# A mixture-of-experts layer: each expert's down product moved from two turns behind its gate product to one

## The chip, the cores and the metric

The kernel runs on one core of one Trainium2 chip. The metric is the device time of one execution of the whole layer in microseconds (us), as the median of the runs made. TensorE (PE) does the matrix products, ScalarE (ACT) and VectorE (DVE) work on their operands and results, GpSimd (POOL) issues the gathers and scatters of token rows, and SyncE (SP) issues the loads of weights. The engines run their own queues in order and meet only at semaphores.

## The reference, cut to what matters

One decoder layer on 1024 tokens of width 1024: attention and a short convolution, an output product, then a layer of 32 experts, of which each token uses two. The change touches the experts alone:

```
def expert_block(args):
    xb, e = args
    return (jax.nn.silu(xb @ w_gate[e]) * (xb @ w_up[e])) @ w_down[e]
```

w_gate and w_up are 1024 x 512 for each expert, w_down is 512 x 1024, all in float32. Each row of the result is weighted by the token's weight for that expert and added to the token's output.

## The kernel before, in words

The front of the kernel (attention, convolution, output product, routing) ends about 637 us into the span; `experts` (line 1505) follows, and the change is in it and in `tile_order` (line 66). Each expert takes up to 96 tokens in one block (SLOTS); what goes beyond that has blocks of its own in `spare_blocks` afterwards.

**The weights** come as tiles of 1 MB, 128 partitions x 2048 floats. Tiles 0 to 3 of an expert hold a quarter each of its gate and up weights, tiles 4 and 5 half each of its down weights. `ORDER` lists all 192 tiles, `PLACE` their place in it. Tile number i is loaded by SP into `raw[i % 12]` as soon as tile i - 12 has been used by PE; ACT rounds it to `w_hi[i % 6]` (`split_hi`, L1592), for which tile i - 6 must have been used; DVE writes what the rounding left, `w_lo`, over `raw` (`split_lo`, L1637). PE multiplies high by high, high by low and low by high parts: 12 matmuls of 512 columns for each tile (L1717, L1719, L1721 for gate and up; L1739, L1741, L1743 for down).

**The turns.** All engines run one loop over turns t. In turn t PE does, in this order: gate tile 0 of expert t; the first half of the transposed rows of expert t + 1 (`turn_rows`, L1693, into bank 4); gate tile 1; the transposes of the hidden rows of expert t - 1 (`turn_hid`, L1701, into bank 5); gate tiles 2 and 3; the second half of the rows of expert t + 1; and the two down tiles of expert t - 2. After gate tile 3 and after down tile 5 PE waits for its own last matmul (L1724, L1746) before it tells ACT.

**The hidden rows** of expert e go: gate and up done (`gated`), ACT's silu (L1600), DVE's product with the up half and the weight (`hidden`, L1647), PE's transposes (L1701), ACT's high part (`round_hid`, L1604), DVE's low part (`low_hid`, L1654), and then PE's down product. ACT copies its result out of banks 2 and 3 (`copy_y`, L1610), and POOL adds it to the output in HBM (`scatter`, L1572), one scatter after the other.

**Order in ACT's and DVE's queues.** In each turn the steps are written at places p = 0 to 5, each behind the split of the p-th tile that PE uses in that turn. Before: the rounding of transposed rows at p = 0 and 3, silu and its product at p = 0 and 1, `copy_y` of expert t - 3 at p = 3, `round_hid` and `low_hid` of expert t - 1 at p = 5. The last two turns (t = 32 and 33) hold no gate product, only what is left over.

**Turns with more.** In turns 4, 7 and 10 DVE also makes parts of the table of the spare blocks (behind split p = 2), and in turn 12 PE sums them and waits for DVE to store the result (SPARE_TURN).

Of the kernel before, what the change touches and what calls it, by code (L numbers as in the profile page):

```python
# [46 lines left out]
E = GROUPS * PER_GROUP  # L47
# [18 lines left out]
def tile_order():  # L66

    order = []
    for e in range(E):
        order += [(e, q) for q in range(4)]  # L70
        order += [(e - 2, q) for q in (4, 5)] if e >= 2 else []
    return order + [(e, q) for e in (E - 2, E - 1) for q in (4, 5)]


ORDER = tile_order()
PLACE = {tile: i for i, tile in enumerate(ORDER)}
# [1428 lines left out]
def experts(nc, sem, s):  # L1505
# [18 lines left out]
    y_ready = sem("y_ready")  # L1524
# [4 lines left out]

    def tile_of(t, p):  # L1530

        return PLACE.get((t, p) if p < 4 else (t - 2, p))

    def half(n):

# [14 lines left out]
    with nc.Block() as block:  # L1550
        @block.sync
        def _(sp):
            for i in range(RING, len(ORDER)):
                sp.wait_ge(s.used, i - RING + 1)
                s.load_tile(sp, i)

        @block.gpsimd
        def _(pool):
            last_row = pool.to_reg(T - 1)

            def gather(e):
                pool.wait_ge(rows_turned[1], e - 1)
                pool.indirect_dma_start(  # L1563
                    out=s.rows[e % 2][:].rearrange("p c q -> p (c q)"), out_offset=None, in_=s.xn2_rows,
                    in_offset=bass.IndirectOffsetOnAxis(ap=s.table_i[:, e:e + 1], axis=0),
                    bounds_check=last_row, oob_is_err=False).then_inc(rows_in[e % 2], 16)

            def scatter(e):
                pool.wait_ge(y_ready, e + 1)
                if e >= 1:  # L1570
                    pool.wait_ge(scattered, e * 16)
                pool.indirect_dma_start(  # L1572
                    out=s.out_rows, out_offset=bass.IndirectOffsetOnAxis(ap=s.table_i[:, e:e + 1], axis=0),
                    in_=s.y_sb[e % 2][:], in_offset=None, bounds_check=last_row, oob_is_err=False,
                    compute_op=ALU.add).then_inc(scattered, 16)

            for e in range(E):
                if e + 2 < E:
                    gather(e + 2)
                if e >= 3:  # L1580
                    scatter(e - 3)
            for e in range(E - 3, E):
                scatter(e)
            pool.wait_ge(scattered, E * 16)

        @block.scalar
        def _(act):
            def split_hi(i):
                if i >= HI:
                    act.wait_ge(s.loaded[i % RING], s.landed(i))  # L1590
                    act.wait_ge(s.used, i - HI + 1)
                    act.copy(s.w_hi[i % HI][:], s.raw[i % RING][:]).then_inc(s.hi_ready, 1)  # L1592

            def round_rows(e, n):
                act.wait_ge(rows_turned[n], e + 1)
                act.copy(s.rT_hi[e % 2][:, half(n), :], turned_rows()).then_inc(rT_hi_ready, 1)  # L1596

            def activate(e):
                act.wait_ge(gated, e + 1)
                act.activation(s.silu[:], ps[0:SLOTS, gate_banks(e), :], ACT.Silu).then_inc(silu_ready, 1)  # L1600

            def round_hid(e):
                act.wait_ge(hid_turned, e + 1)
                act.copy(s.hidT_hi[e % 2][:], turned_hid()).then_inc(hT_hi_ready, 1)  # L1604

            def copy_y(e):
                act.wait_ge(down_done, e + 1)
                if e >= 2:
                    act.wait_ge(scattered, (e - 1) * 16)
                act.copy(s.y_sb[e % 2][:].rearrange("p (a n) -> p a n", a=2), ps[0:SLOTS, 2:4, :]).then_inc(y_ready, 1)  # L1610

            round_rows(0, 0)
            round_rows(0, 1)
            for t in range(E + 2):
                for p in range(6):
                    i = tile_of(t, p)
                    if i is not None:
                        split_hi(i)
                    if p == 0 and 1 <= t < E:
                        round_rows(t, 1)  # L1620
                    if p == 0 and 1 <= t <= E:
                        activate(t - 1)
                    if p == 3 and t + 1 < E:
                        round_rows(t + 1, 0)
                    if p == 3 and t >= 3:
                        copy_y(t - 3)
                    if p == 5 and 1 <= t <= E:
                        round_hid(t - 1)
            copy_y(E - 1)

        @block.vector
        def _(dve):
            own = Order(dve, spare_steps)

            def split_lo(i):
                dve.wait_ge(s.hi_ready, i + 1)
                dve.tensor_tensor(s.w_lo[i % RING][:], s.raw[i % RING][:], s.w_hi[i % HI][:].bitcast(F32),  # L1637
                                  ALU.subtract).then_inc(s.lo_ready, 1)

            def low_rows(e, n):  # L1640
                dve.wait_ge(rT_hi_ready, 2 * e + n + 1)
                dve.tensor_tensor(s.rT_lo[e % 2][:, half(n), :], turned_rows(), s.rT_hi[e % 2][:, half(n), :].bitcast(F32),  # L1642
                                  ALU.subtract).then_inc(rT_lo_ready, 1)

            def hidden(e):
                dve.wait_ge(silu_ready, e + 1)
                dve.scalar_tensor_tensor(s.hid[e % 2][:].rearrange("s c p -> s p c"),  # L1647
                                         s.silu[:].rearrange("s (p c) -> s p c", c=FC), s.table_w[:, e:e + 1],
                                         ps[0:SLOTS, gate_banks(e) + 1, :].rearrange("s (p c) -> s p c", c=FC),
                                         ALU.mult, ALU.mult).then_inc(hid_ready, 1)  # L1650

            def low_hid(e):
                dve.wait_ge(hT_hi_ready, e + 1)
                dve.tensor_tensor(s.hidT_lo[e % 2][:], turned_hid(), s.hidT_hi[e % 2][:].bitcast(F32),  # L1654
                                  ALU.subtract).then_inc(hT_lo_ready, 1)

            for t in range(E + 2):
                for p in range(6):
                    i = tile_of(t, p)
                    if i is not None:  # L1660
                        split_lo(i)
                    if t == 0 and p == 1:
                        low_rows(0, 0)
                        low_rows(0, 1)
                    if p == 0 and 1 <= t < E:
                        low_rows(t, 1)
                    if p == 1 and 1 <= t <= E:
                        hidden(t - 1)
                    if p == 3 and t + 1 < E:
                        low_rows(t + 1, 0)  # L1670
                    if p == 5 and 1 <= t <= E:
                        low_hid(t - 1)
                    if p == 2 and t == SPARE_TURN - 8:
                        spare_places(dve, own.then, s, sp_tab)
                    if p == 2 and t == SPARE_TURN - 5:
                        spare_choices(dve, own.then, s, sp_tab)
                    if p == 2 and t == SPARE_TURN - 2:
                        spare_parts(dve, own.then, s, sp_tab)
                        dve.sem_inc(s.table_parts, 1)
                    if p == 2 and t == SPARE_TURN:  # L1680
                        dve.wait_ge(s.table_summed, 2)
                        spare_columns(dve, own.then, s, sp_tab)
                        dve.sem_inc(columns_ready, 1)

        @block.tensor
        def _(pe):
# [69 lines left out]

            turn_rows(0, 0)
            turn_rows(0, 1)
            for t in range(E + 2):
                if t < E:  # L1760
                    gate_up(t, 0)
                if t + 1 < E:
                    turn_rows(t + 1, 0)
                if t < E:
                    gate_up(t, 1)
                if 1 <= t <= E:
                    turn_hid(t - 1)
                if t == SPARE_TURN:
                    pe.wait_ge(y_ready, t - 2)
                    sum_spare()  # L1770
                    pe.wait_ge(columns_ready, 1)
                if t < E:
                    gate_up(t, 2)
                    gate_up(t, 3)
                if t + 1 < E:
                    turn_rows(t + 1, 1)
                if t >= 2:
                    down(t - 2, 4)
                    down(t - 2, 5)

    x = Shared()
    x.scattered = scattered
# [152 lines left out]
```

## Time and profile before

| | |
|---|---|
| median of 3 runs | 1266.44 us (1266.11 to 1274.25) |
| the profiled execution | 1273.75 us, its span 1271.9 us |
| PE busy over the span | 1132.9 us (89%) |
| DVE, ACT, POOL busy | 839.6 us (66%), 652.8 us (51%), 270.4 us (21%) |
| granted TensorE clock, mean | 0.952 |
| weights and rows read from HBM | 240.55 MB |

The profile page gives the busy time of each engine, the span in 40 slices with the granted clock and the DMA share, the chain that ended last, and the costliest groups of instructions. The trace gives single instructions with their start, their duration and, in brackets, how long their engine had been idle and what released it. A row with "x2" or "x3" holds that many instructions back to back, and the duration is of all of them. An instruction's reported duration reaches beyond the start of the next on the same engine, so chains are best counted from start to start.

### The profile page before, as it was taken

The page shows a single profiled execution, that of the slowest core. Times are in us where ns is not written, and L with a number is a line of the kernel's source. Part 1 is how long each engine was busy: PE and PEld are TensorE (multiplying, and loading weights), DVE is VectorE, ACT ScalarE, POOL GpSimd, SP SyncE. Part 2 cuts the span into 40 slices and gives each one's busy share as a digit, 9 for nine tenths or more (in the row PEclk, how much of TensorE's full clock was granted, in tenths as well). Part 3 has the DMA queues.
Part 4 walks back from the last instruction along what each step waited for, and adds up shares of the span by engine and source line. Part 5 has one row for each costly group of instructions (what it writes and reads, how often), then busy time and mean ns, then how long its engine had stood idle before and what let it go on. Part 6 is the DMA issues. An engine that isn't in the chain of part 4 may idle for free. (4 is left out here: it accounts for less than half of the span.)

```text
span 1271.9 us, 15143 instructions
## 1 busy us (share of the span) xinstructions
PE 1132.9 (89%) x5652; PEld 877.5 (69%) x5652; DVE 839.6 (66%) x911; ACT 652.8 (51%) x869; POOL 270.4 (21%) x397
## 2 busy tenths in 40 slices
PE   3789899999999878998389999999999999999983
PEld 3678788888878767886256666666666666666652
DVE  6546546545565445443578989897888888888851
ACT  5334423442343344221337777776676777777641
POOL 2332232323313312000104121111111111111030
PEclk9789899999999988999589999999999999999997
DMA  8002001200020033226769999999999999999931
GB/s 239 2 1 66 18 17 34 67 18 18 19 65 1 1 133 104 109 106 231 277 205 325 353 364 370 368 365 345 365 363 367 367 357 376 368 364 360 368 95 19
DMA packets 88851, 254.07 MB, mean 200 GB/s; under 512 B 13696, under 2 KB 38288, under 8 KB 80592
## 3 DMA queue, kind: packets, MB, share of 16 engines
q1 hardware_dynamic: 81456, 236.23, 50.7%
q0 software_dynamic: 7328, 16.94, 6.0%
q8 instruction: 43, 0.70, 0.2%
q14 instruction: 24, 0.20, 0.0%
HBM read 240.55 MB, written 20.97 MB: 206 GB/s over the span
## 5 line engine op out<-in xcount | busy, mean ns | idle before, releaser
L1637 DVE TENSOR_TENSOR wlo<-raw,whi 128x2048 fp32r<-128x2048 f32 x192 | 433.7, 2285 | 87.0 <-ACT whi L1592 79.1
L1592 ACT CAST whi<-raw 128x2048 fp32r<-128x2048 f32 x186 | 345.7, 1912 | 0.0
L1717 PE MATMUL banks<-whi,rT_hi 128*96 128x512 f32 x512 | 165.7, 405 | 12.2 <-PE banks L1743 8.8
L1719 PE MATMUL banks<-wlo,rT_hi 128*96 128x512 f32 x512 | 160.6, 395 | 0.0
L1721 PE MATMUL banks<-whi,rT_lo 128*96 128x512 f32 x512 | 160.5, 394 | 0.0
L1596 ACT CAST rT_hi<-banks 128x384 fp32r<-128x384 f32 x64 | 30.7, 479 | 180.2 <-PE banks L1693 180.2
L1572 POOL DMA_INDIRECT out<-y_sb,table_i x32 | 54.7, 1709 | 298.3 <-ACT y_sb L1610 298.0
L1717 PEld LDWEIGHTS banks<-whi,rT_hi 128*96 128x96 f32 x512 | 75.9, 163 | 48.3 <-issue 21.6
L1721 PEld LDWEIGHTS banks<-whi,rT_lo 128*96 128x96 f32 x512 | 83.1, 162 | 36.0
L1719 PEld LDWEIGHTS banks<-wlo,rT_hi 128*96 128x96 f32 x512 | 83.0, 162 | 35.8
L1563 POOL DMA_INDIRECT rows<-xn_rows,table_i x30 | 56.8, 1893 | 218.0 <-PE banks L1693 218.0
L920 PE MATMUL banks<-q_hi,xT_hi 128*128 128x384 f32 x256 | 94.7, 370 | 2.3 <-DVE mixT L797 1.3
L1739 PE MATMUL banks<-whi,hidT_hi 128*96 128x512 f32 x256 | 83.8, 409 | 10.3 <-DVE wlo L1637 10.0
L921 PE MATMUL banks<-q_lo,xT_hi 128*128 128x384 f32 x256 | 90.9, 355 | 0.0
L922 PE MATMUL banks<-q_hi,xT_lo 128*128 128x384 f32 x256 | 90.7, 354 | 0.0
L937 PE MATMUL banks<-xT_hi,c_hi 128*128 128x512 f32 x192 | 76.7, 400 | 6.7 <-issue 5.4
L1743 PE MATMUL banks<-whi,hidT_lo 128*96 128x512 f32 x256 | 81.6, 400 | 0.0
L1741 PE MATMUL banks<-wlo,hidT_hi 128*96 128x512 f32 x256 | 81.6, 400 | 0.0
L939 PE MATMUL banks<-xT_hi,c_lo 128*128 128x512 f32 x192 | 74.9, 390 | 0.0
L938 PE MATMUL banks<-xT_lo,c_hi 128*128 128x512 f32 x192 | 74.8, 390 | 0.0
L610 ACT ACTIVATE qk_sq<-banks 128x256 f32<-128x256 f32 x32 | 12.3, 384 | 120.0 <-PE banks L922 120.0
L729 DVE TENSOR_REDUCE qk_ss<-qk_sq 128x4 f32<-128x256 f32 x32 | 13.5, 421 | 78.3 <-ACT qk_sq L610 78.3
(243 smaller groups left out, 2016.2 us busy)
## 6 DMA issues: line engine op xcount, KB each, us to landing
raw<-in_w_gate SPq DMA_DIRECT2D x128, 512.0 KB, 6.5
raw<-in_w_up SPq DMA_DIRECT2D x128, 512.0 KB, 11.7
raw<-in_w_down SPq DMA_DIRECT2D x64, 1024.0 KB, 11.5
q_raw<-in_w_in SPq DMA_DIRECT2D x12, 512.0 KB, 6.0
c_raw<-in_w_in SPq DMA_DIRECT2D x12, 512.0 KB, 3.8
x_all<-in_x SPq DMA_DIRECT2D x8, 512.0 KB, 7.4
wo_raw<-in_w_out SPq DMA_DIRECT2D x2, 2048.0 KB, 11.5
x_again<-in_x SPq DMA_DIRECT2D x8, 512.0 KB, 4.1
```

Of the source, the lines that this page charges most:

```text
L920: pe.matmul(o, s.xT_hi[:, c, cols], s.q_hi[:, c, :], start=(c == 0), stop=False)
L921: pe.matmul(o, s.xT_hi[:, c, cols], s.q_lo[:, c, :], start=False, stop=False)
L922: ins = pe.matmul(o, s.xT_lo[:, c, cols], s.q_hi[:, c, :], start=False, stop=(c == KC - 1))
L937: pe.matmul(ps[:, 6, :], w_hi[:, c, :], s.xT_hi[:, c, cols], start=(c == 0), stop=False)
L1592: act.copy(s.w_hi[i % HI][:], s.raw[i % RING][:]).then_inc(s.hi_ready, 1)
L1637: dve.tensor_tensor(s.w_lo[i % RING][:], s.raw[i % RING][:], s.w_hi[i % HI][:].bitcast(F32), ALU.subtract).then_inc(s.lo_ready, 1)
L1717: pe.matmul(ps[0:SLOTS, bank + g, :], s.rT_hi[e % 2][:, c, :], hi[:, g, c2, :], start=(c == 0), stop=False)
L1719: pe.matmul(ps[0:SLOTS, bank + g, :], s.rT_hi[e % 2][:, c, :], lo[:, g, c2, :], start=False, stop=False)
L1721: ins = pe.matmul(ps[0:SLOTS, bank + g, :], s.rT_lo[e % 2][:, c, :], hi[:, g, c2, :], start=False, stop=(c == KC - 1))
L1739: pe.matmul(ps[0:SLOTS, 2 + n, :], s.hidT_hi[e % 2][:, c, :], hi[:, c2, n * 512:(n + 1) * 512], start=(c == 0), stop=False)
L1741: pe.matmul(ps[0:SLOTS, 2 + n, :], s.hidT_hi[e % 2][:, c, :], lo[:, c2, n * 512:(n + 1) * 512], start=False, stop=False)
L1743: ins = pe.matmul(ps[0:SLOTS, 2 + n, :], s.hidT_lo[e % 2][:, c, :], hi[:, c2, n * 512:(n + 1) * 512], start=False, stop=(c == FC - 1))
```

## The change

The down product of expert e now runs in turn e + 1, not e + 2. The order of the weight tiles moves with it, and so do the steps on ACT, DVE and POOL: `copy_y` takes expert t - 2 at p = 2, `round_hid` and `low_hid` stand at p = 3, behind the rounding of the rows, and POOL scatters expert e - 2. The loops have one turn fewer. No instruction, load or wait is added or removed; the same ones stand in another order.

```
-        order += [(e - 2, q) for q in (4, 5)] if e >= 2 else []
-    return order + [(e, q) for e in (E - 2, E - 1) for q in (4, 5)]
+        order += [(e - 1, q) for q in (4, 5)] if e >= 1 else []
+    return order + [(E - 1, q) for q in (4, 5)]
...
-        return PLACE.get((t, p) if p < 4 else (t - 2, p))
+        return PLACE.get((t, p) if p < 4 else (t - 1, p))
...
-                if e >= 3:
-                    scatter(e - 3)
-            for e in range(E - 3, E):
+                if e >= 2:
+                    scatter(e - 2)
+            for e in range(E - 2, E):
                 scatter(e)
...
-                    if p == 3 and t >= 3:
-                        copy_y(t - 3)
-                    if p == 5 and 1 <= t <= E:
+                    if p == 2 and t >= 2:
+                        copy_y(t - 2)
+                    if p == 3 and 1 <= t <= E:
                         round_hid(t - 1)
...
-                    if p == 5 and 1 <= t <= E:
+                    if p == 3 and 1 <= t <= E:
                         low_hid(t - 1)
...
-                    pe.wait_ge(y_ready, t - 2)
+                    pe.wait_ge(y_ready, t - 1)
...
-                if t >= 2:
-                    down(t - 2, 4)
-                    down(t - 2, 5)
+                if t >= 1:
+                    down(t - 1, 4)
+                    down(t - 1, 5)
```

All loops over `range(E + 2)` become `range(E + 1)`.

**ACT's queue in a steady turn.** Before, from the rounding of the second half of the rows (first row below) to that of the next turn (last row):

```order
L1596 CAST rT_hi_174<-banks 128x384
L1600 ACTIVATE silu<-banks 96x512
L1592 CAST whi_169<-raw_151 128x2048
L1592 CAST whi_170<-raw_152 128x2048
L1592 CAST whi_171<-raw_153 128x2048
L1596 CAST rT_hi_175<-banks 128x384
L1610 COPY y_sb_186<-banks 96x1024
L1592 CAST whi_166<-raw_142 128x2048
L1592 CAST whi_167<-raw_143 128x2048
L1604 CAST hidT_hi_181<-banks 128x384
L1592 CAST whi_168<-raw_144 128x2048
L1596 CAST rT_hi_175<-banks 128x384
```

Now, the same stretch:

```order
L1596 CAST rT_hi_174<-banks 128x384
L1600 ACTIVATE silu<-banks 96x512
L1592 CAST whi_171<-raw_153 128x2048
L1592 CAST whi_166<-raw_142 128x2048
L1610 COPY y_sb_185<-banks 96x1024
L1592 CAST whi_167<-raw_143 128x2048
L1596 CAST rT_hi_175<-banks 128x384
L1604 CAST hidT_hi_181<-banks 128x384
L1592 CAST whi_168<-raw_144 128x2048
L1592 CAST whi_169<-raw_145 128x2048
L1592 CAST whi_170<-raw_146 128x2048
L1596 CAST rT_hi_175<-banks 128x384
```

Gate tiles 1 and 2 stand before the copy of y and gate tile 3 behind it; the hidden rows are rounded before the two down tiles, which had stood in front of them.

**DVE's queue in a steady turn.** Before, from the low part of the rows' first half to the product of the next turn (raw_142 and raw_143 hold the down tiles here, the next two hold gate tiles 0 and 1):

```order
L1642 TENSOR_TENSOR rT_lo_177<-banks,rT_hi_175 128x384
L1637 TENSOR_TENSOR wlo_154<-raw_142,whi_166 128x2048
L1637 TENSOR_TENSOR wlo_155<-raw_143,whi_167 128x2048
L1654 TENSOR_TENSOR hidT_lo_183<-banks,hidT_hi_181 128x384
L1637 TENSOR_TENSOR wlo_156<-raw_144,whi_168 128x2048
L1642 TENSOR_TENSOR rT_lo_177<-banks,rT_hi_175 128x384
L1637 TENSOR_TENSOR wlo_157<-raw_145,whi_169 128x2048
L1647 SCALAR_TENSOR_TENSOR hid_178<-silu,table_w,banks 96x128x4
```

Now, from gate tile 3 (raw_143) to the product of the next turn; the down tiles are in raw_144 and raw_145:

```order
L1637 TENSOR_TENSOR wlo_155<-raw_143,whi_167 128x2048
L1642 TENSOR_TENSOR rT_lo_177<-banks,rT_hi_175 128x384
L1654 TENSOR_TENSOR hidT_lo_183<-banks,hidT_hi_181 128x384
L1637 TENSOR_TENSOR wlo_156<-raw_144,whi_168 128x2048
L1637 TENSOR_TENSOR wlo_157<-raw_145,whi_169 128x2048
L1637 TENSOR_TENSOR wlo_158<-raw_146,whi_170 128x2048
L1642 TENSOR_TENSOR rT_lo_177<-banks,rT_hi_175 128x384
L1637 TENSOR_TENSOR wlo_159<-raw_147,whi_171 128x2048
L1647 SCALAR_TENSOR_TENSOR hid_178<-silu,table_w,banks 96x128x4
```

The low part of the hidden rows (L1654) came behind the down tiles' splits and now comes in front of them.

**ACT's queue at the end.** Before, from the silu of the last expert:

```order
L1600 ACTIVATE silu<-banks 96x512
L1610 COPY y_sb_186<-banks 96x1024
L1592 CAST whi_168<-raw_150 128x2048
L1592 CAST whi_169<-raw_151 128x2048
L1604 CAST hidT_hi_181<-banks 128x384
L1610 COPY y_sb_185<-banks 96x1024
L1592 CAST whi_170<-raw_152 128x2048
L1592 CAST whi_171<-raw_153 128x2048
L1610 COPY y_sb_186<-banks 96x1024
```

Now:

```order
L1592 CAST whi_168<-raw_150 128x2048
L1592 CAST whi_169<-raw_151 128x2048
L1600 ACTIVATE silu<-banks 96x512
L1610 COPY y_sb_185<-banks 96x1024
L1604 CAST hidT_hi_181<-banks 128x384
L1592 CAST whi_170<-raw_152 128x2048
L1592 CAST whi_171<-raw_153 128x2048
L1610 COPY y_sb_186<-banks 96x1024
```

The down tiles of expert 30 (whi_168, whi_169) stood behind a copy of y and now stand ahead of the last silu; those of expert 31 stand behind a copy of y in both.

## Rows read from the trace of the kernel before

**Rows 1.** Page: the span, and each engine's busy time, share, instructions.
```profile
span 1271.9 us, 15143 instructions
PE 1132.9 (89%) x5652; PEld 877.5 (69%) x5652; DVE 839.6 (66%) x911; ACT 652.8 (51%) x869; POOL 270.4 (21%) x397
```

**Rows 2.** Stretch: us; busy PE, PEld, DVE, ACT, POOL (count); clock, DMA share, GB/s.
```profile
700.00:1212.00 512.00, 498.58 (x2342) 343.52 (x2341) 443.49 (x302) 372.95 (x304) 82.53 (x53) 1.00 1.01 364
```

**Rows 3.** Timeline, PE, one steady turn (t = 5): start, us, what, [idle before].
```profile
728.34 0.67 PE L1717 MATMUL banks<-whi,rT_hi 128*96 128x512 f32 x2 [0.30 <-PE banks L1743]
...
734.26 0.49 PE L1701 MATMUL banks<-ident,hid 96*128 96x96 f32 x4
...
740.75 0.68 PE L1739 MATMUL banks<-whi,hidT_hi 128*96 128x512 f32 x2
...
746.82 0.67 PE L1717 MATMUL banks<-whi,rT_hi 128*96 128x512 f32 x2 [0.30 <-PE banks L1743]
```

**Rows 4.** Timeline, ACT, the same turn.
```profile
723.39 5.52 ACT L1592 CAST whi<-raw 128x2048 fp32r<-128x2048 f32 x3
731.69 0.48 ACT L1596 CAST rT_hi<-banks 128x384 fp32r<-128x384 f32 x1 [2.78 <-PE banks L1693]
732.06 1.01 ACT L1610 COPY y_sb<-banks 96x1024 f32<-96x1024 f32 x1
732.97 3.72 ACT L1592 CAST whi<-raw 128x2048 fp32r<-128x2048 f32 x2
...
741.00 0.48 ACT L1596 CAST rT_hi<-banks 128x384 fp32r<-128x384 f32 x1 [2.14 <-PE banks L1693]
```

**Rows 5.** Timeline, DVE, the same turn.
```profile
728.33 1.15 DVE L1647 SCALAR_TENSOR_TENSOR hid<-silu,table_w,banks 96x512 f32<-96x512 f32 x1
729.32 4.47 DVE L1637 TENSOR_TENSOR wlo<-raw,whi 128x2048 fp32r<-128x2048 f32 x2
733.72 0.54 DVE L1642 TENSOR_TENSOR rT_lo<-banks,rT_hi 128x384 fp32r<-128x384 f32 x1
...
739.33 0.55 DVE L1654 TENSOR_TENSOR hidT_lo<-banks,hidT_hi 128x384 fp32r<-128x384 f32 x1
```

**Rows 6.** DMA issues, 700 to 1200 us: count, KB each, median us to landing.
```profile
raw<-in_w_up SPq DMA_DIRECT2D x106, 512.0 KB, 12.5
```

**Rows 7.** Timeline, DVE, turn 7: first table step, and the split behind the last.
```profile
767.65 0.69 DVE L1471 TENSOR_TENSOR which<-own_e,iota_e 128x512 f32<-128x512 f32 x1
...
771.59 2.29 DVE L1637 TENSOR_TENSOR wlo<-raw,whi 128x2048 fp32r<-128x2048 f32 x1
```

**Rows 8.** Timeline, PE, starts of turn 2, of its gate tile 1, and of turn 3.
```profile
670.41 0.68 PE L1717 MATMUL banks<-whi,rT_hi 128*96 128x512 f32 x2
...
675.80 0.70 PE L1717 MATMUL banks<-whi,rT_hi 128*96 128x512 f32 x2 [2.07 <-DVE wlo L1637]
...
691.38 0.67 PE L1717 MATMUL banks<-whi,rT_hi 128*96 128x512 f32 x2 [0.30 <-DVE wlo L1637]
```

**Rows 9.** Timeline, DVE, turns 1 and 2, where it waits.
```profile
667.10 2.28 DVE L1637 TENSOR_TENSOR wlo<-raw,whi 128x2048 fp32r<-128x2048 f32 x1
671.17 0.56 DVE L1642 TENSOR_TENSOR rT_lo<-banks,rT_hi 128x384 fp32r<-128x384 f32 x1 [1.79 <-ACT rT_hi L1596]
```

**Rows 10.** Timeline, all engines, from the end of turn 31 on.
```profile
1229.92 0.62 PE L1743 MATMUL banks<-whi,hidT_lo 128*96 128x512 f32 x2
...
1231.58 3.70 ACT L1592 CAST whi<-raw 128x2048 fp32r<-128x2048 f32 x2
...
1233.51 4.49 DVE L1637 TENSOR_TENSOR wlo<-raw,whi 128x2048 fp32r<-128x2048 f32 x2 [7.13 <-ACT whi L1592]
...
1235.94 1.14 PE L1739 MATMUL banks<-whi,hidT_hi 128*96 128x512 f32 x2 [4.58 <-DVE wlo L1637]
...
1249.74 1.14 PE L1739 MATMUL banks<-whi,hidT_hi 128*96 128x512 f32 x2 [5.41 <-DVE wlo L1637]
...
1257.48 0.63 PE L1743 MATMUL banks<-whi,hidT_lo 128*96 128x512 f32 x2
```

More of the change, by code:

```diff
@@ L1613, in _ @@
             round_rows(0, 1)
-            for t in range(E + 2):
+            for t in range(E + 1):
                 for p in range(6):
@@ L1655, in low_hid @@
                                   ALU.subtract).then_inc(hT_lo_ready, 1)
-            for t in range(E + 2):
+            for t in range(E + 1):
                 for p in range(6):
@@ L1758, in _ @@
             turn_rows(0, 1)
-            for t in range(E + 2):
+            for t in range(E + 1):
                 if t < E:
```

## The prediction

> **What bounds the kernel now.** The page comes first: PE is busy for 89% of the span, DVE for 66%, ACT for 51% [rows 1]. The change lies in the expert turns, so the next view is the busy time of that stretch: from 700 to 1212 us PE is busy for 498.58 of 512 us at a granted clock of 1.00, the 2.4 GHz level, while DVE has 443.49 and ACT 372.95 us [rows 2]. The DMA share is 1.01 there, so a second resource could be the bound; it has to be excluded, which I do below.
>
> Then the timeline of one steady turn. It begins on PE at 728.34 and the next at 746.82, 18.48 us later. Nothing in it waits for another engine; the 0.30 us ahead of each is PE's wait for its own last matmul [rows 3]. Counting from the turn's start, PE turns the hidden rows at 5.92, starts gate tile 2 at about 6.20 and the first down tile at 12.41. The down block holds PE for 18.48 - 12.41 = 6.07 us. Since each gate tile takes a good 2.8 us, gate tile 3 starts at about 9.02. ACT and DVE work ahead of PE: ACT idles 2.78 and 2.14 us in the turn, both times until PE has transposed rows, and never for a landing [rows 4].
>
> So a steady turn is bound by PE's own work, which the change leaves as it is. PE is idle for reasons that the change can touch in two places only: the start (turn 2) and the end (turns 32 and 33).
>
> **The end, before.** The last down matmuls of turn 31 end at 1229.92 + 0.62 = 1230.54. Only then does ACT copy y, and behind that copy stands the high part of the next down tile, from 1231.58; DVE's low part starts at 1233.51 and PE at 1235.94: a gap of 5.40 us. The same is repeated behind expert 30's product, with a gap of 5.41 us; the last product then starts at 1249.74 and ends at 1257.48 + 0.63 = 1258.11, after 8.37 us [rows 10]. Both products begin slow: the first pair of matmuls takes 1.14 us, where pairs at full clock take 0.62. At full clock the block takes 6.07 - 0.30 = 5.77 us [rows 3].
>
> **The end, after.** Expert 30's product runs in turn 31 right behind gate tile 3, its tiles split long before. That makes turn 31 end where turn 31 of before ended, plus one down block: 1230.54 + 6.07 = 1236.61. Then one gap is left. Its chain: ACT's copy of y, released 0.13 us after the last matmul, takes 0.91 us start to start (732.06 to 732.97 [rows 4]); that puts the cast of before at 1.04, as 1231.58 - 1230.54 shows. Now `round_hid` stands between them. It needs PE's transposes, which PE starts 0.30 us after the end and finishes by about 0.8, so ACT doesn't wait; it adds 0.37 us, start to start, of its 0.48. The cast starts at 1.41, and from cast to PE are 4.36 us (1231.58 to 1235.94), so PE starts 5.77 after the end: 1242.38. The product starts slow again, since its gap is as long as the two of before; I take the 8.37 us. End at 1250.75, against 1258.11: **7.36 us less**. What follows (the last copy and scatter) stays.
>
> **The start.** Turn 2 goes from 670.41 to 691.38, 20.97 us, where a steady turn with the same work (it has the down block of expert 0) takes 18.48. The excess, **2.49 us**, is mostly one stall of 2.07 us ahead of gate tile 1 [rows 8]. DVE made gate tile 0's low part at 667.10, then idled 1.79 us until ACT had the next rows at 671.17 [rows 9]; neither had anything to split in that time, as turn 1 has no down tiles. Now it has them. DVE makes them from 667.10 and about 669.3, and gate tile 0 of turn 2 from 671.5. PE runs the down block of expert 0 from 670.41 to 676.48 and needs gate tile 1 at 679.57. DVE has it at about 671.5 + 2.20 + 0.55 + 2.43 = 676.7 (a split 2.20 start to start, rows' low part 0.55, start of a split to its user 2.43). The stall goes; nothing takes its place.
>
> **The price in a steady turn.** Before, `round_hid` and `low_hid` had a whole turn until their down product. Now the chain is: transposes at 5.92, ACT released about 0.53 later at 6.45, the hidden rows' high part 0.37, the down tile's cast and low part 4.36 as at the end, so the tile is ready at 11.18. PE wants it at 12.41. **The margin is 1.23 us**; past it, each of 31 turns pays.
> The rest of the queues, from the same rows. ACT: casts of gate tiles 1 and 2 from -4.95 (723.39) to -1.3; the copy of y then waits until -0.18, when the down block before is done; gate tile 3 from 0.73 to 2.65; the rows at 3.35 as before; `round_hid` at 6.45; three casts from 6.82, 1.84 apart, the last ended at 12.4; the rows of the next turn at 12.66 as before (741.00) [rows 4]. That is 0.3 us spare, and what lies behind it has several. DVE: low part of hidden rows at 6.96, down tiles at 8.75 and 10.95, gate tile 0 at 13.15, rows at 15.35, gate tile 1 at 15.9, product at 18.1 (0.99 to the next [rows 5]), gate tile 2 at 0.6 of the next turn, gate tile 3 at 2.8, ready at 5.2 and wanted at 9.02. DVE still idles some 2.5 us a turn, in front of the hidden rows and of the down tile. I charge a steady turn **0**.
> Turns 4, 7 and 10 put table steps behind gate tile 2, 771.59 - 767.65 = 3.94 us in turn 7, the longest [rows 7]. Gate tile 3 then starts at 6.75 on DVE and is ready at 9.18 for 9.02: 0.16 us, once; the other two are 0.2 us shorter. Then rows and hidden rows (1.1) and the down tile ready at 12.5 for 12.41, another 0.1. I charge **0.2** in all; the bound from the other side is 0.5 for each. Turn 12 stops PE for the table's sum in both kernels; behind it DVE has gate tile 3, rows, hidden rows and a down tile, 2.20 + 0.55 + 0.55 + 2.43 = 5.7 us, and PE needs the last after 12.41 - 6.20 = 6.2. Nothing.
> SP's loads and POOL's scatters: a tile's buffer comes free at the same place as before, twelve tiles ahead, some 37 us. Loads land 12.5 us after issue [rows 6]; ACT now reads the down tile 5.6 us before PE, so some 28 us after its load's issue. The scatter leaves about 3 us earlier in its turn, behind the same gather. Nothing.
>
> **The sum.** 7.36 + 2.49 - 0.2 = 9.65 us. The profiled execution had a span of 1271.9 and a time of 1273.75, 7.3 above the median of 1266.44; the turns are the same work in each, so I take the difference from either: span 1262.2, median **1256.8 us** (0.76% less).
>
> **Bounds.** The last product's speed isn't known: at full clock throughout it takes 5.77, which gives 2.6 less (1254.2); at half throughout 11.5, which gives 3.2 more (1260.0). The Trainium skill, "TensorE: Matmul & The Clock Gate" (section on what's actually happening), says that the same kernel may show 6, 11 or 14 slow matmuls from run to run; these rows don't show such a spread.
>
> **Rivals.**
> *The loads are the bound, and the start's gain is given back* (1259.3). The DMA share of 1.01 speaks for it, ACT's never waiting for a landing against. PE would catch up with the loads and lose the 2.49 us again. The Trainium skill, "DMA: Bandwidth & Descriptors" (where 436 GB/s comes from), puts HBM's limit for a core near 358 GB/s. The trace has 364 over the stretch [rows 2], so it disagrees in size, and by that rule no margin would be left and this rival would be the forecast.
> *The end doesn't shorten* (1264.2): the chain behind expert 31's transposes is longer than read, or expert 30's product stalls in turn 31 for the same 7 us. Against it: its splits stand ahead of the silu in ACT's queue.
> *Slower: the down product waits in each turn.* Place: L1739 of each turn for the low part, L1637. It decides from 1.23 us of lateness; the gains are gone at 1.23 + 9.65 / 31 = 1.54. If the chain were 2.0 us longer, 31 x 0.77 = 24 us, less 9.65: 1281. For it: ACT and DVE are now tied to the transposes only two PE tiles ahead. Against: durations vary by hundredths in these rows, and ACT idles before the transposes come.
> *More than 1% faster* (under 1253.8): the slow start of the last product vanishes and the end has something more.
>
> **How the numbers follow.** Forecast 0.62; start given back 0.14; end not shortened 0.07; slower 0.09; more than 1% 0.08. The executions before lie 8 us apart (1266.11 to 1274.25), and a median of the new kernel may fall towards the upper one, so the range reaches past the second rival's side to 1265 above and to 1253 below; the forecast's own range is 1254 to 1260. A difference within 1% (12.7 us) is about what a measurement of this kernel can't tell from no change. Faster by over 1%: 0.08; within 1%: 0.83; slower: 0.09.
>
> **What would show it.** Right: turn length 18.48; turn 2 without a stall at L1717; L1739 waiting for DVE once, at the end, some 5 us; the gap from the last matmul of expert 30 to the next down matmul 5.8; span near 1262. Wrong: waits of L1739 for L1637 in steady turns; ACT idle for a landing; more than 0.5 us in turns 4, 7, 10; two gaps at the end.

## The result, and the profile after

| | before | changed |
|---|---|---|
| median of 9 executions each | 1268.99 us (1266.11 to 1274.25) | 1261.89 us (1258.35 to 1263.61) |
| ratio, 95% interval | | 0.9934 (0.9911 to 0.9956) |
| the profiled execution: time, span | 1273.75, 1271.9 us | 1258.35, 1256.5 us |
| first row transposes of the experts start at | 637.32 us | 632.04 us |
| from there to the end of the last matmul | 620.79 us | 610.68 us |

The change makes the kernel 0.66% faster, with an interval from 0.44 to 0.89%; the two medians lie 7.1 us apart. The two profiled spans differ by 15.4 us, which is too much: 5.3 us of it lie ahead of the experts, in code that the change doesn't touch. The fair measure of the mechanism is the last line, called the **stretch** below. It is 10.1 us shorter.

The page of the changed kernel, engine totals: the counts are those of [rows 1]. PE is busy for 7.2 us less, ACT for 6.6 us more and POOL for 41 us more. In the expert turns an issue of the scatter takes POOL 3.56 us on average, where it took 1.71 (32 issues in each); what makes it longer was not tried. POOL idles for most of the span, and PE waits for it nowhere in these turns.

```profile
span 1256.5 us, 15143 instructions
PE 1125.7 (90%) x5652; PEld 872.1 (69%) x5652; DVE 839.3 (67%) x911; ACT 659.4 (52%) x869; POOL 311.7 (25%) x397
```

**The start.** PE's timeline of the changed kernel: the second rows' transposes of turn 1, then the starts of turns 2 and 3 (start, duration, what, idle before). The last two answer to [rows 8].

```profile
664.84 0.52 PE L1693 MATMUL banks<-ident,rows 96*128 96x96 f32 x4
...
671.20 0.67 PE L1717 MATMUL banks<-whi,rT_hi 128*96 128x512 f32 x2 [0.30 <-DVE wlo L1637]
...
689.68 0.67 PE L1717 MATMUL banks<-whi,rT_hi 128*96 128x512 f32 x2 [0.30 <-PE banks L1743]
```

Turn 2 takes 689.68 - 671.20 = 18.48 us, where it took 20.97. The stall of 2.07 us is gone.

**A steady turn.** ACT's timeline of turn 2, which began at 671.20, to be read beside [rows 4], and DVE's rows of the same turn.

```profile
674.55 0.48 ACT L1596 CAST rT_hi<-banks 128x384 fp32r<-128x384 f32 x1 [0.70 <-PE banks L1693]
677.66 0.48 ACT L1604 CAST hidT_hi<-banks 128x384 fp32r<-128x384 f32 x1 [2.62 <-PE banks L1701]
...
683.87 0.48 ACT L1596 CAST rT_hi<-banks 128x384 fp32r<-128x384 f32 x1 [0.31 <-PE banks L1693]
```
```profile
678.17 0.56 DVE L1654 TENSOR_TENSOR hidT_lo<-banks,hidT_hi 128x384 fp32r<-128x384 f32 x1 [1.13 <-ACT hidT_hi L1604]
679.98 6.69 DVE L1637 TENSOR_TENSOR wlo<-raw,whi 128x2048 fp32r<-128x2048 f32 x3 [1.25 <-ACT whi L1592]
```

Counted from the turn's start, the rows stand at 3.35, the hidden rows at 6.46 after 2.6 us of idling, and the next rows at 12.67 after 0.31. The low part stands at 6.97 and the down tile at 8.78 on DVE.

**The end.** All engines of the changed kernel from the last matmuls of turn 31 on, against [rows 10].

```profile
1228.02 0.63 PE L1743 MATMUL banks<-whi,hidT_lo 128*96 128x512 f32 x2
1228.78 1.01 ACT L1610 COPY y_sb<-banks 96x1024 f32<-96x1024 f32 x1 [5.47 <-PEq L1747]
...
1229.69 0.48 ACT L1604 CAST hidT_hi<-banks 128x384 fp32r<-128x384 f32 x1
1230.06 3.70 ACT L1592 CAST whi<-raw 128x2048 fp32r<-128x2048 f32 x2
...
1231.99 4.49 DVE L1637 TENSOR_TENSOR wlo<-raw,whi 128x2048 fp32r<-128x2048 f32 x2 [1.24 <-ACT whi L1592]
1234.43 1.14 PE L1739 MATMUL banks<-whi,hidT_hi 128*96 128x512 f32 x2 [4.96 <-DVE wlo L1637]
...
1242.10 0.62 PE L1743 MATMUL banks<-whi,hidT_lo 128*96 128x512 f32 x2
```

One gap is left, from 1228.65 to 1234.43. The last product runs 8.3 us. The busy times from the last matmul of expert 30 on (us; busy PE, PEld, DVE, ACT, POOL; granted clock, DMA share, GB/s) show why it is slow: 4.4 us behind the end of that matmul, with only four transposes on PE in between, the clock goes to 0.50, the 1.2 GHz level, and stays there for 6.8 us. The first 1.3 of these lie in the gap and 5.5 in the product.

```profile
1228.70:1233.10 4.40, 0.52 (x4) 0.37 (x4) 1.66 (x2) 4.32 (x4) 1.40 (x1) 1.00 0.24 22
1233.10:1239.90 6.80, 5.47 (x13) 3.75 (x14) 3.39 (x2) 0.66 (x1) 0.00 (x0) 0.50 0.15 29
1239.90:1242.70 2.80, 2.80 (x12) 1.63 (x11) 0.00 (x0) 0.00 (x0) 0.00 (x0) 0.99 0.00 0
```

### The profile page after: what moved, and what is told of

Same layout as the page of the kernel before. It is cut to its first block and busy times, and to the rows that moved or that the text cites. A ratio compares the mean times of both kernels' runs of the same rounds, so it can differ in the third digit from the quotient of the medians.

```text
span 1256.5 us, 15143 instructions
## 1 busy us (share of the span) xinstructions
PE 1125.7 (90%) x5652; PEld 872.1 (69%) x5652; DVE 839.3 (67%) x911; ACT 659.4 (52%) x869; POOL 311.7 (25%) x397
## 3 DMA queue, kind: packets, MB, share of 16 engines
HBM read 240.55 MB, written 20.97 MB: 208 GB/s over the span
## 5 line engine op out<-in xcount | busy, mean ns | idle before, releaser
L1572 POOL DMA_INDIRECT out<-y_sb,table_i x32 | 113.9, 3559 | 208.4 <-ACT y_sb L1610 208.4
L1563 POOL DMA_INDIRECT rows<-xn_rows,table_i x30 | 39.5, 1316 | 255.9 <-PE banks L1693 242.7
L1739 PE MATMUL banks<-whi,hidT_hi 128*96 128x512 f32 x256 | 82.6, 404 | 5.3 <-DVE wlo L1637 5.0
```

Of the source, the lines that this page charges most:

```text
L1572: pool.indirect_dma_start(out=s.out_rows, out_offset=bass.IndirectOffsetOnAxis(ap=s.table_i[:, e:e + 1], axis=0), in_=s.y_sb[e % 2][:], in ...
L1739: pe.matmul(ps[0:SLOTS, 2 + n, :], s.hidT_hi[e % 2][:, c, :], hi[:, c2, n * 512:(n + 1) * 512], start=(c == 0), stop=False)
```

## Experiments on the end and the start

All gains of the sum lay at the two ends of the expert turns. That leaves a question that the result can't answer: is it the shorter lag that gains them, or only the order of the queues there? The first three runs ask it. They were timed beside the kernel before (median 1272.41 us there) and the changed kernel, four executions of each edit. Every stretch below comes from one profiled execution.

### tail_two_behind

The kernel before, with the splits of the last four down tiles taken out of turns 32 and 33:

```diff
-                    if i is not None:
+                    if i is not None and not (t >= E):
                         split_hi(i)
...
                         activate(t - 1)
+                    if p == 0 and t == E:
+                        split_hi(PLACE[E - 1, 4])
+                        split_hi(PLACE[E - 1, 5])
...
                         round_hid(t - 1)
+                    if p == 5 and t == E - 1:
+                        split_hi(PLACE[E - 2, 4])
+                        split_hi(PLACE[E - 2, 5])
```

and the same with `split_lo` on DVE, behind `hidden` and `low_hid`.

> The kernel before (down product two experts behind), with one thing changed: the splits of the last four down tiles are moved ahead of the copies of y on ScalarE and VectorE (expert 30's behind the hidden rows of turn 31, expert 31's behind the last silu). The stretch from the first row transposes of the experts to the end of the last matmul is 620.8 us in the kernel before and 610.7 in the changed one. Theory A (the end is long because the splits stand behind a copy of y, whatever the lag is): each of the two gaps of 5.40 shrinks to copy plus signals, about 1.3 us, and since PE idles so little both products run at full clock, 5.77 instead of 8.4: stretch 607.3, 13.5 us less than before and 3.4 less than the changed kernel. Rival B (it is the lag of two experts itself that costs the time at the end): little changes, 618 to 621.

Measured: stretch 607.5 us, ratio to before 0.9897 (0.9863 to 0.9931). The timeline of this kernel, first matmul of expert 30's product and of expert 31's, and what stands between:

```profile
1226.46 1.01 ACT L1610 COPY y_sb<-banks 96x1024 f32<-96x1024 f32 x1 [1.86 <-PEq L1759]
...
1227.57 0.68 PE L1751 MATMUL banks<-whi,hidT_hi 128*96 128x512 f32 x2 [0.41 <-issue]
...
1233.46 1.01 ACT L1610 COPY y_sb<-banks 96x1024 f32<-96x1024 f32 x1 [5.61 <-DMA out<-y_sb,table_i]
1234.57 0.67 PE L1751 MATMUL banks<-whi,hidT_hi 128*96 128x512 f32 x2 [1.24 <-ACT y_sb L1610]
```

Each gap has shrunk to the copy of y, and no pair of matmuls is slow (0.67 and 0.68 for the first). Theory A holds to 0.2 us. The kernel with the old lag and a better end has a shorter stretch than the changed kernel.

### start_tail_two_behind

In addition, gate tile 1 of turn 2 is split behind gate tile 0, ahead of the rounding of that turn's rows:

```diff
-                    if i is not None and not (t >= E):
+                    if i is not None and not (t >= E) and (t, p) != (2, 1):
                         split_hi(i)
+                    if t == 2 and p == 0:
+                        split_hi(PLACE[2, 1])
```

and the same on DVE.

> The kernel before with the end's splits moved as in the run before, and with gate tile 1 of turn 2 split ahead of the rounding of turn 2's rows. Theory A: the 2.49 us of turn 2 go as well: stretch 604.8 us, 16.0 less than before, ratio about 0.9874, with the down product still two experts behind. Rival B: the start's gain needs the down product in turn 1: stretch as in the run before, 607.3.

Measured: stretch 605.3 us, ratio 0.9878 (0.9843 to 0.9914). PE's timeline of this kernel, the starts of turns 2 and 3:

```profile
665.09 0.68 PE L1733 MATMUL banks<-whi,rT_hi 128*96 128x512 f32 x2
...
683.58 0.68 PE L1733 MATMUL banks<-whi,rT_hi 128*96 128x512 f32 x2 [0.30 <-PE banks L1759]
```

Turn 2 takes 18.49 us, where it took 20.98 in tail_two_behind: the whole 2.49. The start doesn't need the early down product either. The total misses its 604.8 by 0.5. Turn 12 was 1.4 us longer, by a slow clock (below, under the hardware), and the very first matmuls 1.2 us shorter than in the kernel before; the other 0.3 stands in turns 14 and 17, of 18.65 us each. Single turns longer by some 0.1 us stand in most of the profiles, the kernel before's included, and not in the same turns in all.

### tail_one_behind

The changed kernel, with expert 31's splits moved ahead of the last copy:

```diff
-                    if i is not None:
+                    if i is not None and not (t >= E):
                         split_hi(i)
...
                         activate(t - 1)
+                    if p == 0 and t == E:
+                        split_hi(PLACE[E - 1, 5])
...
                         round_hid(t - 1)
+                    if p == 5 and t == E - 1:
+                        split_hi(PLACE[E - 1, 4])
```

and the same with `split_lo` on DVE.

> The changed kernel with the splits of expert 31's down tiles moved ahead of the last copy of y (tile 4 at the end of turn 31, tile 5 behind the last silu). Theory A: the gap of 5.78 us shrinks to what the hidden rows and the copy of y take, about 2.2 us, and the last product runs at full clock, 5.8 instead of 8.3: stretch 604.6, 6.1 less than the changed kernel, and the same as start_tail_two_behind within 0.5 us. Rival B (one expert behind is worth something of its own): at least 3 us below start_tail_two_behind.

Measured: stretch 605.1 us, ratio 0.9871 (0.9839 to 0.9902), median 1255.54 us. Between the two products stand only the copy and the hidden rows:

```profile
1231.61 1.01 ACT L1610 COPY y_sb<-banks 96x1024 f32<-96x1024 f32 x1 [3.51 <-PEq L1755]
1231.78 0.52 PE L1709 MATMUL banks<-ident,hid 96*128 96x96 f32 x4 [0.30 <-PE banks L1751]
1232.52 0.48 ACT L1604 CAST hidT_hi<-banks 128x384 fp32r<-128x384 f32 x1
...
1233.03 0.56 DVE L1658 TENSOR_TENSOR hidT_lo<-banks,hidT_hi 128x384 fp32r<-128x384 f32 x1 [0.92 <-ACT hidT_hi L1604]
1233.64 0.70 PE L1747 MATMUL banks<-whi,hidT_hi 128*96 128x512 f32 x2 [1.34 <-DVE hidT_lo L1658]
```

PE idles for 1.34 us instead of 4.96, and the product behind takes 5.8 us instead of 8.3. This version beats both kernels. It is also level with start_tail_two_behind: 605.1 against 605.3. So the shorter lag has no worth of its own that these stretches show, to some tenths of a microsecond; it gained what a queue order at the two ends could have gained with the old lag.

### after_again

The changed kernel in the same rounds, no edit.

> The changed kernel as it is, beside the others on one chip: stretch 610.7 us from first row transposes to last matmul, as in its first profile; ratio to the kernel before 0.992 to 0.994.

Measured: stretch 610.8 us, ratio 0.9924 (0.9899 to 0.9949), median 1262.51. Its span was 1263.7 us, 7.2 more than in its first profile, with the experts starting at 638.91 instead of 632.04: 6.9 us of the difference lie ahead of them.

## Experiments on the margin in a steady turn

These runs and those on the loads were executed once each, so they are compared by their stretches and turns alone.

### chain_plus_1 and chain_plus_2

The rival on the slow side rested on a margin of 1.23 us that no run had shown. One and two idle copies make the chain longer:

```diff
                         round_hid(t - 1)
+                        for k in range(2 if t > SPARE_TURN else 0):
+                            act.copy(s.idle[k][:], s.y_sb[(t - 1) % 2][:])
```

(`range(1 ...)` in chain_plus_1; the targets are 4 KB each at 195 and 199 KB, unused after turn 12.)

> The changed kernel with one idle ScalarE copy (96 x 1024, about 0.95 us) behind the rounding of the hidden rows in turns 13 to 32, writing to a buffer that nobody reads. It lengthens the chain from the transposes to the first down matmul. By the margin of 1.23 us read from the rows: no cost in the turns, 0.95 at the end, stretch 611.6. If the margin were smaller or ScalarE itself near its bound, each of 19 turns would pay up to 0.95, stretch up to 630.

> As chain_plus_1 with two idle copies, about 1.9 us in all. By the margin of 1.23 us: turns 13 to 31 pay 0.65 each, a turn is 19.15 us, the wait stands at the first down matmul for the low part; the end pays 1.9; stretch 625. If ScalarE were the bound: 1.9 in each turn, stretch 648. If the chain didn't matter: 612.6.

Measured: 611.55 us and 625.11 us. With one copy every turn from 13 on still takes 18.47 to 18.51 us. With two each takes 19.15 to 19.18. The waits of PE in chain_plus_2 (waiter, what it waited for, us in total, times, longest):

```profile
PE banks L1742 <- DVE wlo L1640: 9.6, 19, 1.1
```

and one such turn, from the hidden rows to the first down matmul:

```profile
1103.70 0.48 ACT L1605 CAST hidT_hi<-banks 128x384 fp32r<-128x384 f32 x1 [2.62 <-PE banks L1704]
...
1107.91 6.69 DVE L1640 TENSOR_TENSOR wlo<-raw,whi 128x2048 fp32r<-128x2048 f32 x3 [3.14 <-ACT whi L1593]
...
1110.35 0.67 PE L1742 MATMUL banks<-whi,hidT_hi 128*96 128x512 f32 x2 [0.47 <-DVE wlo L1640]
```

The cost per turn is 19.16 - 18.48 = 0.68 us. Two copies of about 0.95 less 0.68 leave 1.2 us: the margin is as read. ACT's idling ahead of the hidden rows is still 2.62 us, so it was not ACT that became the bound.

### hidden_late

The changed kernel, with `round_hid` and `low_hid` behind both down tiles again:

```diff
-                    if p == 3 and 1 <= t <= E:
+                    if p == 5 and 1 <= t <= E:
                         round_hid(t - 1)
...
-                    if p == 3 and 1 <= t <= E:
+                    if p == 5 and 1 <= t <= E:
                         low_hid(t - 1)
```

> The changed kernel with one part undone: the rounding of the hidden rows and its low part stand at p = 5 again, behind the splits of the two down tiles. Theory A (the place in the steady turn is free, there is slack on both sides): steady turn 18.48 us as before, DVE has the low part ready about 10.7 us into the turn for a use at 12.41; only the end changes, where the cast of the down tile no longer stands behind the hidden rows: gap 5.41 instead of 5.78, stretch 610.3 against 610.7. Rival B (p = 3 is what makes one expert behind possible): the down product waits in each turn, stretch over 615.

Measured: stretch 618.98 us. Both theories missed. The steady turns are free, at 18.48. But PE waits for the hidden rows' low part in five places:

```profile
PE banks L1739 <- DVE hidT_lo L1654: 11.7, 5, 7.2
```

Four are in turns 1, 4, 7 and 10, which are 1.26, 1.34, 1.49 and 1.35 us longer than in the changed kernel. The rows of turn 7 show the mechanism in a turn with table steps: a split released by the last table step, the rows, two more splits, and only then the hidden rows.

```profile
780.09 2.29 DVE L1637 TENSOR_TENSOR wlo<-raw,whi 128x2048 fp32r<-128x2048 f32 x1
782.30 0.55 DVE L1642 TENSOR_TENSOR rT_lo<-banks,rT_hi 128x384 fp32r<-128x384 f32 x1
782.77 4.48 DVE L1637 TENSOR_TENSOR wlo<-raw,whi 128x2048 fp32r<-128x2048 f32 x2
...
787.17 0.55 DVE L1654 TENSOR_TENSOR hidT_lo<-banks,hidT_hi 128x384 fp32r<-128x384 f32 x1
...
787.77 0.71 PE L1739 MATMUL banks<-whi,hidT_hi 128*96 128x512 f32 x2 [1.31 <-DVE hidT_lo L1654]
```

I had placed the low part at 10.1 us of a steady turn (done at 10.7), and it is there; with 3.5 to 3.8 us of table steps ahead of it, it starts at 13.1 to 13.3, for a use at 12.41. Turn 1 has no table steps. There DVE has built up no lead yet: it had waited 6.23 us for the rows that ACT rounds early in that turn, and the low part starts at 13.75. The fifth wait is the end, where it stands behind both splits: 7.16 us of idling instead of 4.96. The product behind that longer idle was the faster one, though. The busy times from the last matmul of expert 30 on, as above:

```profile
1243.60:1247.60 4.00, 0.52 (x4) 0.37 (x4) 1.08 (x1) 3.92 (x3) 1.40 (x1) 1.00 0.18 13
1247.60:1254.40 6.80, 2.87 (x7) 1.97 (x8) 3.88 (x3) 1.06 (x2) 0.00 (x0) 0.50 0.20 36
1254.40:1258.60 4.20, 4.20 (x19) 2.65 (x17) 0.00 (x0) 0.00 (x0) 0.00 (x0) 1.00 0.00 0
```

The slow stretch is as long as in the changed kernel, 6.8 us at 0.50, and begins 4.0 us behind the last full matmul, where it was 4.4. But as the product starts later, only 2.9 us of it fall on the product, which takes 7.1 us instead of 8.3. The account of the 8.3 us that this stretch is longer by: 5.4 in the four turns, 1.0 at the end (2.2 of idling less 1.2 of clock), 1.5 in turn 12, whose clock was slow in this execution, and 0.3 in small pieces of late turns, where PE waits for no other engine. So the place p = 3 is worth 6.4 us, the turns and the end together; without it the change would gain some 3.7 of its 10.1. A split of the second down tile has no business ahead of what the first down matmul needs.

## Experiments on the loads

### loads_late and loads_late_2

```diff
-                sp.wait_ge(s.used, i - RING + 1)
+                sp.wait_ge(s.used, i - RING + 5)
```

(+ 3 in loads_late_2, that is two tiles later instead of four.)

> The changed kernel with each load of a weight tile issued four tiles later (12.3 us). By the slack read from the rows (some 28 us from issue to the cast, of which 12.5 for the load) nothing changes: stretch 610.7, ScalarE never waits for a landing. If the loads were the bound, as a DMA share of 1.01 suggests, ScalarE and then PE would wait for landings in the steady turns, and the stretch would be 10 us longer or more.

Measured: stretch 621.98 us, so this expectation fell. From turn 1 to turn 17 the turns are as long as in the changed kernel, to 0.1 us; from turn 18 to 29 they take 18.9 to 21.1. ACT's waits between 640 and 1240 us (the first of them in turn 8, before PE feels them):

```profile
ACT whi L1592 <- DMA raw<-in_w_up: 87.6, 58, 3.1
```

The down tiles' loads of this run, 1060 to 1160 us (count, KB each, median us to landing), and those of the changed kernel in the same stretch:

```profile
raw<-in_w_down SPq DMA_DIRECT2D x10, 1024.0 KB, 17.1
```
```profile
raw<-in_w_down SPq DMA_DIRECT2D x12, 1024.0 KB, 13.5
```

> The changed kernel with each load issued two tiles later, 6.2 us; four tiles later the stretch was 622.0 us and ScalarE waited 87.6 us for landings, where I had read some 28 us from issue to cast and expected none. If the loads are only late by their own queue (17 us to landing in that run, against 13.5 late in the changed kernel), two tiles leave 28 - 6.2 = 22 us for 13.5 to 17: no wait, stretch 610.7. If the sustained rate of the loads is itself below what PE asks for in 18.48 us, waits come here too, only later in the run: stretch 612 to 618.

Measured: stretch 611.5 us, no wait of ACT for a landing. Turn 12 was 1.6 us longer and the first matmuls 1.1 us shorter than in the changed kernel; without those two it is 611.1.

So two tiles of lateness are hidden and four are not, in one execution each, on two chips. My slack, some 28 us from issue to cast less 12.5 for the landing, would have hidden five. What it missed is that the landing time is not a constant of the load: in the changed kernel a down tile's median goes from 7.9 us at 660 to 760 us to 13.5 at 1060 to 1160, and in loads_late to 17.1. The DMA share is no help here: from 950 to 1180 us it is 1.01 in loads_late, which moved 355 GB/s, and in the changed kernel, which moved 367. The loads are no bound of either kernel, but close behind PE. Whether the slower landings of loads_late come from the late issue or from the execution is left open. Against the late issue alone speaks loads_late_2, also late, whose median is 8.8 us at 660 to 760 us and 11.2 at 1060 to 1160, below the changed kernel's 13.5 there, while loads_late has 12.0 at 660 to 760 already.

## Why the prediction was right, point by point

- **The bound.** A steady turn is 18.48 us before and after, and PE waits for no other engine in it. Right. The dismissal of the loads was right in its result and careless in its working: the slack was taken from one median of the landing time [rows 6]. A limit near 358 GB/s did not bind here: the kernel moved 364 GB/s before, and the changed one 367 from 950 to 1180 us, with no wait of ACT for a landing.
- **The start, 2.49 us.** Measured: before, turn 3 starts 54.06 us after the first row transposes, which with the added down block of 6.07 would be 60.13; now it starts at 57.64. That is 2.49.
- **Table turns, 0.2 us.** Turn 7 shows 18.53 against 18.48, and turns 4 and 10 nothing: 0.05 us, where I had 0.2. A term that was too large, and too small to matter. In the middle the changed kernel even came out ahead by 0.2 us, because the one before has turns of 18.57 and 18.63 in its profile; no run tells what those are.
- **The end, 7.36 us.** The end is 7.4 us shorter. The gap was forecast at 5.77 and is 5.78. The last product took 8.3 us, where 8.37 was assumed. The step rested on taking over the slow product of before, and the granted clock of 0.50 behind the gap bears it out. The Trainium skill, "TensorE: Matmul & The Clock Gate" (what's actually happening), has the array at 1.2 GHz after idling; here it is so behind an idle of 4.96 us and not behind one of 1.34. But that the forecast came so close is in part luck: the page speaks of a count of slow matmuls that changes from run to run, I wrote that the rows don't show such a spread, and the runs show one. Behind the same idle of 4.96 us the last product took 8.30, 8.26, 7.80 and 8.42 us (the changed kernel, after_again, loads_late, loads_late_2).
- **The sum.** 9.65 us forecast, 10.1 in the stretch, 8.4 in the timed ratio (0.66% of 1268.99, interval 5.6 to 11.3).
- **The time itself.** 1256.8 forecast, 1261.89 measured. That is 5.1 us off, outside the forecast's own range of 1254 to 1260 and inside the wide one of 1253 to 1265. Half of it is the base: 1266.44 was the median of three executions, while nine give 1268.99, and 1268.99 - 9.65 = 1259.3. The other 2.6 us are the difference, 9.65 against the 7.1 between the medians; the interval of the ratio, 5.6 to 11.3 us, holds both. That they come from the part ahead of the experts, whose length spreads by 8 us in the profiles, is likely and not shown, since the other executions have no trace. The wide range, which was set for the spread of the executions, is what held the time.
- **The slow rival.** Its threshold was right (1.2 us, from chain_plus_2), and so were its place, L1739 for the low part, and its price.
- **The loads as a rival.** Not this time: the start's gain was kept. But loads_late shows that this rival deserved its chance more than the argument from ACT's idle times allowed.
- **What the prediction did not see.** It costed the moved `round_hid` and `low_hid` by asking what the new place costs, and never what the old place would. hidden_late shows 6.4 us. The forecast held because the new place is the right one, which the working never asked; there it was lucky.

## What to carry to other kernels

When a pipeline's lag is changed and the steady turn is bound by one engine's own work, look for the gain at its two ends, and count there what stands ahead of what in each queue: operands split behind a copy that waits for the last product cost a gap that no lag cures. A margin read start to start from a steady turn held here to a tenth of a microsecond (1.23 us read, 1.22 measured), but it has to be read in the turns with extra work, and in the first, too. A transfer's time to landing was no constant of the load here, so slack worked out from one median of it was too large.

## What the runs showed of the hardware that I had not expected

- **The part ahead of the experts comes in two lengths.** In eleven profiles of identical code ahead of the experts, these started at 632.0 to 634.5 us in seven and at 637.3 to 640.2 in four. In the changed kernel's two profiles 6.6 us of the difference between 632.04 and 638.91 are there between 123 and 430 us, most of it in three steps of 2.2, 2.5 and 1.4 us, near 134, 362 and 428 us of the longer one. At the first two PE waits for an operand from ACT for 2.43 and 2.58 us, where it waited 1.09 and 1.60, and at all three its clock is low behind the wait. Over all eleven the granted clock from 83 to 440 us averages 0.98 in each of the four long profiles and 0.99 in each of the seven short ones. Why ACT is later and the clock lower in some executions, no run tells. The difference is about as large as the change's gain, and it hides in the median of few executions.
- **In turn 12 the clock falls in some executions.** There PE runs 32 matmuls of 42 columns in 2.84 us and then idles 0.76 us, in every kernel. The turn is 22.17 us in eight of eleven profiles and 23.59, 23.71 and 23.73 in three (start_tail_two_behind, hidden_late, loads_late_2). Whether the small matmuls or the pause bring it on, no run tells apart. The busy times of start_tail_two_behind, one of the three, show a clock of 0.66 over the 5 us behind the last of the small matmuls:

```profile
859.10:864.10 5.00, 4.24 (x13) 2.86 (x13) 4.72 (x6) 1.44 (x1) 0.00 (x0) 0.66 0.81 265
```

and those of tail_two_behind, one of the eight, 1.00 at the same place:

```profile
862.70:867.70 5.00, 4.25 (x19) 3.00 (x20) 4.76 (x6) 1.41 (x1) 0.00 (x0) 1.00 0.88 274
```

- **A longer idle made the product behind it faster, not slower.** In the eight profiles with a long gap at the end (nine gaps, as the kernel before has two), the clock is at 0.50 for 6.8 us each time. This stretch begins 3.4 to 5.1 us behind the last full matmul, whatever the length of the gap. So the later the product starts, the less of it is slow: 8.4 us behind idles of 4.58 and 5.41 (the kernel before), 7.8 to 8.4 behind 4.96, 8.0 behind 5.90 (chain_plus_1), 7.7 behind 6.84 (chain_plus_2), 7.1 behind 7.16 (hidden_late), against 5.8 at full clock. The total of gap and product still grows with the gap.
